# Row gathers of a retrieval layer: all query groups ahead of the first weighted sum, query weights in eight 1 MB loads

## The reference, cut to what matters

```python
def peer_ffn(xn, w_q, sub_keys, u, v):
    def block(xb):                                   # 128 tokens
        q = (xb @ w_q).reshape(PEER_BLOCK, PEER_HEADS, 2, PEER_HALF)
        s = jnp.einsum('thpd,hpnd->thpn', q, sub_keys).astype(jnp.float32)
        s_top, i_top = lax.top_k(s, PEER_TOPK)
        cand = s_top[:, :, 0, :, None] + s_top[:, :, 1, None, :]
        ...
        best, pos = lax.top_k(cand, PEER_TOPK)
        expert = jnp.take_along_axis(cand_idx, pos, axis=-1)
        g = jax.nn.softmax(best, axis=-1)
        act = jax.nn.gelu(jnp.einsum('td,thkd->thk', xb, u[expert]), approximate=False)
        return jnp.einsum('thk,thkd->td', (g * act).astype(xb.dtype), v[expert])
...
mem_kv = _rmsnorm(mem, norm_mem) @ w_mem_kv          # second layer, keys and values of the memory branch
```

## Time and profile before

| | us |
|---|---|
| median of 3 runs | 1346.45 (1339.59 to 1346.51) |
| the profiled execution | 1344.95 |
| its span on the core | 1343.2 |
| TensorE busy | 1111.8 |
| VectorE busy | 776.9 |
| ScalarE busy | 466.1 |
| GpSimd busy | 294.1 |
| granted clock of TensorE, mean | 0.928 of full |

### The profile page before, as it was taken

One profiled execution on the slowest core, in us unless ns is written; L12 is line 12 of the kernel. 1 busy time (PEld: TensorE's weight loads), 2 busy tenths in 40 slices (PEclk: granted clock), 3 DMA queues, 4 the chain that ended last, 5 costly groups with the idle time before them and its releaser, 6 DMA issues.

```text
span 1343.2 us, 13221 instructions
## 1 busy us (share of the span) xinstructions
PE 1111.8 (83%) x4936; PEld 745.6 (56%) x4936; DVE 776.9 (58%) x1528; ACT 466.1 (35%) x979; POOL 294.1 (22%) x313
## 2 busy tenths in 40 slices
PE   9999996749448677685976868676799999999997
PEld 9889784534213233232432323232498989888886
DVE  6587536123275665857567484344476664665665
ACT  5556211112032322322322232122448534465443
POOL 0052101130244433253342424133100000000001
PEclk9999998879779989799897979898899999999999
DMA  6453454356799999999999999999254423435533
GB/s 208 174 189 126 143 187 188 125 219 281 279 366 422 421 421 422 421 422 421 422 422 421 422 420 422 417 356 391 95 188 156 158 98 124 157 127 188 192 122 110
DMA packets 57665, 363.98 MB, mean 271 GB/s; under 512 B 6768, under 2 KB 9088, under 8 KB 16128
## 3 DMA queue, kind: packets, MB, share of 16 engines
q0 software_dynamic: 36864, 268.45, 48.6%
q1 hardware_dynamic: 20272, 94.48, 19.6%
q10 hardware_dynamic: 464, 0.20, 0.1%
HBM read 361.01 MB, written 2.10 MB: 270 GB/s over the span
## 4 chain that ended last, share of the span: by engine, by line
PE 59%; DMA 19%; DVE 12%; ACT 4%; POOL 3%; issue 2%; POOLq 0%; DVEq 0%; ACTq 0%
PE ps L2075 19%; PE ps L1912 18%; DMA big<-in_uv,big 11%; PE ps L1878 9%; DMA ring<-in_uv,big 4%; PE ps L1834 3%; DMA actT<-in_uv,big 2%; DVE big L1475 2%; PE ps L1963 2%; ACT big L993 1%; POOL ring L778 1%; POOL big L778 1%; PE ps L2025 1%; DVE lo L1270 1%; PE ps L1792 1%
## 5 line engine op out<-in xcount | busy, mean ns | idle before, releaser
L2075 PE MATMUL ps<-big 128*128 128x512 f32 x552 | 275.5, 647 | 124.3 <-ACT big L993 124.3
L2075 PEld LDWEIGHTS ps<-big 128*128 128x128 f32 x552 | 111.5, 206 | 278.0 <-ACT big L993 144.2
L1475 DVE CUSTOM_DVE_ANT_0 big<-big,ps 128x1024 f32<-128x1024 f32 x138 | 166.6, 1220 | 156.6 <-DMA big<-in_uv,big 154.1
L2075 PE MATMUL ps<-ring,big 128*128 128x512 f32 x336 | 166.5, 636 | 75.1 <-ACT big L993 69.4
L1912 PE MATMUL ps<-hi,x 128*128 128x512 f32 x704 | 227.0, 397 | 1.2 <-DVE lo L1270 1.0
L778 POOL DMA_INDIRECT big<-in_uv,big x138 | 131.0, 949 | 297.5 <-PE ps L2075 162.7
L985 ACT ACTIVATE big<-big 128x4 f32<-128x4 f32 x64 | 13.1, 205 | 487.6 <-DVE big L1475 487.6
L1270 DVE TENSOR_TENSOR lo<-raw,hi 128x2048 fp32r<-128x2048 f32 x60 | 139.2, 2321 | 74.1 <-ACT hi L859 73.8
L1475 DVE CUSTOM_DVE_ANT_0 ring<-ring,ps 128x1024 f32<-128x1024 f32 x84 | 101.9, 1220 | 138.0 <-DMA ring<-in_uv,big 138.0
L2075 PEld LDWEIGHTS ps<-ring,big 128*128 128x128 f32 x336 | 67.9, 206 | 168.8 <-issue 89.2
L1912 PEld LDWEIGHTS ps<-hi,x 128*128 128x128 f32 x704 | 133.7, 190 | 30.2 <-issue 2.2
(11 more groups left out here) (369 smaller groups left out, 1340.3 us busy)
## 6 DMA issues: line engine op xcount, KB each, us to landing
raw<-in_pieces SPq DMA_DIRECT2D x61, 1024.0 KB, 4.8
ring<-in_peer_w_q SPq DMA_DIRECT2D x4, 2048.0 KB, 8.0
big<-in_up SPq DMA_DIRECT2D x4, 2048.0 KB, 8.5
big<-in_uv,big POOLq DMA_INDIRECT x138
ring<-in_w_mem_kv SPq DMA_DIRECT2D x1, 2048.0 KB, 18.0
ring<-in_uv,big POOLq DMA_INDIRECT x84
resid<-in_x SPq DMA_DIRECT2D x2, 512.0 KB, 4.7
raw<-in_pieces SPq DMA_DIRECT2D x2, 512.0 KB, 8.9
```

The source lines that it names most:

```text
L1475: ins = dve.tensor_tensor_reduce(out=row, in0=row, in1=hn_ps[n], scale=1.0, scalar=0.0, op0=ALU.mult, op1=ALU.add, accum_out=dots[:, n, s: ...
L2075: ins = pe.matmul(ps[:, 4 + 2 * n + half, :], diag[:, s % DIAGS], row_home[home_of[k]][:, D + half * TILE:D + (half + 1) * TILE], start=(s ...
```

## The change

The query weights come as eight loads of 1 MB, one for each group, in three half slots of the ring (ring0, ring1, ring2) in turn: load i + 3 waits for group i. `mv` comes as two loads of 1 MB into ring0 and ring1. TensorE computes all eight query groups and their key scores before any weighted sum; from group 2 on the key scores come one group late, and the memory steps of groups 2 to 5 move behind, the last of them now after batch 7. ScalarE's hand-written order follows. The homes change: rows 4, 5 and 6 take ring3, ring4 and ring5, free since the output projection, row 7 takes ring2 (after group 5), row 8 actT (after group 7), rows 9 to 11 query0, query1 and keys (after the last key scores), row 24 mixT, rows 40 to 42 memT, ring0 and ring1 (after mv1), row 48 mkv; each other row takes the home that has been in use longest.

```diff
+WQ_HOMES = 3
...
-        tiles1 = [("wq0", wtile("peer_w_q", 0)), ("wq1", wtile("peer_w_q", TILE)),
-                  ("wq2", wtile("peer_w_q", 2 * TILE)), ("wq3", wtile("peer_w_q", 3 * TILE)),
-                  ("mv", wtile("w_mem_kv_2", TILE))]
...
+        def wq_view(i):
+            return ring_half[i % WQ_HOMES].rearrange("p (c n) -> p c n", c=KC)
+
+        def mv_view(c):
+            return ring_half[c // HALF].rearrange("p (c n) -> p c n", c=HALF)[:, c % HALF]
...
+        def query_used(i):
+
+            return group_done, group_no["wq00"] + i + 1
...
-        FIRST_ROW = {"early0": 0, "early1": 0, "early2": 0, "early3": 0, "ring4": 4, "ring5": 4, "ring0": 8, "ring1": 8, "actT": 8,
-                     "query0": 8, "query1": 8, "keys": 8, "mixT": 8, "memT": 24, "ring2": 24, "ring3": 24, "mkv": 32}
+        FIRST_ROW = {"early0": 0, "early1": 0, "early2": 0, "early3": 0, "ring3": 4, "ring4": 5, "ring5": 6, "ring2": 7,
+                     "actT": 8, "query0": 9, "query1": 10, "keys": 11, "mixT": 24, "memT": 40, "ring0": 40, "ring1": 41, "mkv": 48}
...
-            for k, (name, make) in enumerate(tiles1):
-                if k == 0:
-                    sp.wait_ge(piece_lo, NP1)
-                elif k == 1:
+            sp.wait_ge(piece_lo, NP1)
+            for i in range(PH):
+                if i == 2:
                     sp.wait_ge(wout_done, 4)
-                elif k >= RING:
-                    sp.wait_ge(*tile_used(tiles1[k - RING][0]))
-                dst, src = make(k % RING)
-                sp.dma_start(dst, src).then_inc(tile_loaded[k % RING], 16)
+                elif i >= WQ_HOMES:
+                    sp.wait_ge(*query_used(i - WQ_HOMES))
+                src = t["peer_w_q"][:, i * T:(i + 1) * T].rearrange("(c p) n -> p c n", p=P)
+                sp.dma_start(wq_view(i), src).then_inc(query_then_mv_loaded[i % WQ_HOMES], 16)
+            for k in range(2):
+                sp.wait_ge(*query_used(PH - 2 + k))
+                sp.dma_start(ring_half[k].rearrange("p (c n) -> p c n", c=HALF), w_mem[:, HALF * k:HALF * (k + 1), TILE:2 * TILE]).then_inc(query_then_mv_loaded[k], 16)
...
+            mv_used = (group_done, group_no["mv1"] + 1)
+            home_ready = {"ring3": (wout_done, 4), "ring4": (wout_done, 4), "ring5": (wout_done, 4), "ring2": query_used(5),
+                          "actT": query_used(PH - 1), "query0": (sub_done, PH), "query1": (sub_done, PH), "keys": (sub_done, PH),
+                          "mixT": (group_done, group_no["mk1"] + 1), "memT": mv_used, "ring0": mv_used, "ring1": mv_used, "mkv": (hq0a_then_mkv_moved, 32)}
...
             for i in range(PH):
                 out_query(i)
-                out_scores(i)
-                if i == 2:
+                if i == 3:
                     exponentials(0)
-                if i == 4:
+                if i >= 3:
+                    out_scores(i - 1)
+                elif i < 2:
+                    out_scores(i)
+                if i == PH - 2:
                     exponentials(1)
-                    weigh(0)
-                if i == 6:
-                    weigh(1)
-            out_memory("mk1")
-            for b in range(2, BATCHES):
+            out_scores(PH - 1)
+            for b in range(BATCHES):
                 weigh(b)
                 if b == 4:
+                    out_memory("mk1")
+                if b == 6:
                     out_memory("mv0")
-                if b == 6:
+                if b == 8:
                     out_memory("mv1")
...
             for i in range(PH):
-                features(f"wq{i // 2}", actT, (i % 2,))
-                if i < 6:
+                query_features(i)
+                if i < 2:
                     memory(19 + 2 * i, 21 + 2 * i)
-                if i == 0:
-                    pe.wait_ge(cols_then_mem_loaded, 96)
-                key_scores(i)
-                if i == 4:
-                    weighted_rows(0)
-                if i == 6:
-                    weighted_rows(1)
-            memory(31, 32)
-            for b in range(2, BATCHES):
+                    if i == 0:
+                        pe.wait_ge(cols_then_mem_loaded, 96)
+                    key_scores(i)
+                elif i > 2:
+                    key_scores(i - 1)
+            memory(23, 25)
+            key_scores(PH - 1)
+            for b in range(BATCHES):
                 weighted_rows(b)
-                if b < 6:
-                    memory(24 + 4 * b, 28 + 4 * b)
+                if b == 2:
+                    memory(25, 28)
+                if 3 <= b < 8:
+                    memory(4 * b + 16, 4 * b + 20)
```

More of the change, by code:

```diff
@@ L222, in build @@
         memT_done = sem("memT_done")
-        tile_loaded = [sem(f"tile_loaded{i}") for i in range(RING)]
+        tile_loaded = [sem(f"tile_loaded{i}") for i in range(2)]
+        query_then_mv_loaded = [sem(f"query_then_mv_loaded{i}") for i in range(WQ_HOMES)]
         consts_made = sem("consts_made")
@@ L269, in build @@
         t["mkv_keep"] = nc.dram_tensor("mkv_keep", (P, 2048), F32, kind="Internal").ap()
[L272 to L284 removed]
+        loads_p = [len(range(s, NP1, 2)) for s in range(2)]
         tokens_of = ["hi", "gv", "hgate", "ggate", "wo0", "wo1", "dnz", "gmu", "gmv", "gmz", "swz", "xmz"]
@@ L304, in piece_loads @@
             k, s = load_no[name], raw_slot(name)
-            return 16 * (k // 2 + 1 if k < NP1 else loads1[s] + (k - NP1) // 2 + 1)
+            return 16 * (k // 2 + 1 if k < NP1 else loads_p[s] + (k - NP1) // 2 + 1)
         def raw_piece(name):
@@ L318, in build @@
         up_order = [(k % 2, k // 2) for k in range(4)]
-        def slot(name):
-            return tile_no[name] % RING
-        def tile_view(name):
-            return ring[:, slot(name), :].rearrange("p (c n) -> p c n", c=KC)
+        ring_half = [ring[:, k // 2, (k % 2) * 2 * D:(k % 2 + 1) * 2 * D] for k in range(6)]
+        def wq_view(i):
+            return ring_half[i % WQ_HOMES].rearrange("p (c n) -> p c n", c=KC)
+        def mv_view(c):
+            return ring_half[c // HALF].rearrange("p (c n) -> p c n", c=HALF)[:, c % HALF]
         groups1 = ["hq0", "hq1", "hf0", "hf1", "gqk0", "gqk1", "glow", "hi0", "hi1", "gv0", "gv1",
@@ L372, in build @@
         EARLY = 15872
-        ring_half = [ring[:, k // 2, (k % 2) * 2 * D:(k % 2 + 1) * 2 * D] for k in range(6)]
         row_home = {f"early{k}": big[:, EARLY + 2 * D * k:EARLY + 2 * D * (k + 1)] for k in range(3)}
         row_home["early3"] = past_actT[:]
-        for k in (4, 5, 0, 1):
+        for k in (3, 4, 5, 2):
             row_home[f"ring{k}"] = ring_half[k]
@@ L1813, in transpose_to_tiles @@
                             ins.then_inc(transposed, 1)
-            def need(name):
-                pe.wait_ge(tile_loaded[slot(name)], 16 * (loads_p[slot(name)] + tile_no[name] // RING + 1))
             def bank_free(g):
@@ L1822, in bank_free, with query_features @@
                     pe.wait_ge(group_out, same[-1] + 1)
-            def features(name, xT, subs):
-                need(name)
-                w = tile_view(name)
-                for s in subs:
-                    g = f"{name}{s}"
-                    bank_free(g)
-                    for a in range(2):
-                        f0 = (2 * s + a) * P
-                        for c in range(KC):
-                            ins = pe.matmul(ps[:, gbank(g), a * T:(a + 1) * T], w[:, c, f0:f0 + P], xT[:, c, :], start=(c == 0), stop=(c == KC - 1))
-                    ins.then_inc(group_done, 1)
-            def tokens(name, xT):
-                need(name)
-                w = tile_view(name)
-                for n in range(NT):
-                    g = f"{name}{n}"
-                    bank_free(g)
+            def query_features(i):
+                pe.wait_ge(query_then_mv_loaded[i % WQ_HOMES], 16 * (i // WQ_HOMES + 1))
+                w = wq_view(i)
+                g = f"wq{i // 2}{i % 2}"
+                bank_free(g)
+                for a in range(2):
                     for c in range(KC):
-                        ins = pe.matmul(ps[:, gbank(g), :], xT[:, c, n * P:(n + 1) * P], w[:, c, :], start=(c == 0), stop=(c == KC - 1))
-                    ins.then_inc(group_done, 1)
+                        ins = pe.matmul(ps[:, gbank(g), a * T:(a + 1) * T], w[:, c, a * P:(a + 1) * P], actT[:, c, :], start=(c == 0), stop=(c == KC - 1))
+                ins.then_inc(group_done, 1)
             FRESH = {"hq0": 0, "dnq0": 16}
@@ L2018, in memory @@
                         if g == "mv0":
-                            need("mv")
+                            for half in range(2):
+                                pe.wait_ge(query_then_mv_loaded[half], 16 * (len(range(half, PH, WQ_HOMES)) + 1))
                     if k < 32:
@@ L2024, in memory @@
                         n = (k - 32) // KC
-                        ins = pe.matmul(ps[:, gbank(g), :], memT[:, c, n * P:(n + 1) * P], tile_view("mv")[:, c], start=(c == 0), stop=(c == KC - 1))
```

(1 more changed line is left out.)

16 lines of the change are left out of this document (1 added, 15 removed).

## The result

The changed kernel takes 1287.42 us, median of 4 runs (1284.83 to 1290.32), beside 1346.48 us for the kernel before, also 4 runs (1339.59 to 1347.63). The ratio is 0.9572, 95% interval 0.9532 to 0.9613. The profiled run of the changed kernel took 1285.52 us with a span of 1283.8 us, 59.4 us less than the span of before.

The account below looks back on a forecast made before the run. Gather bytes at 421 GB/s were taken as the bound. From 259.5, 607.6 for 244 rows, 2.5 store, 1.5 dark and 20.4 tail gave 891.5, 61.3 us sooner; span 1282 and 1.75 around it, forecast 1285 us, range 1272 to 1302.

Parts of the forecast that it names:

- The bound: Whole gather stretch: once gathers run at full rate, only their bytes count, 2.49 us a row at 421 GB/s.
- Dark time as the measure: Gather stretch: time the DMA engines stand idle sets the gain, 77.0 us before and 13.8 after.
- Rival 2: Query loads starve beside the gathers: load 6 also late, group 6 slips some 9 us, 1294 us; chance 0.06.
- Load 7: Last query-weight load, issued beside rows 0 to 6: lands with the last queued byte at 232.3, costing 2.4 us.
- Group 7: Last query group on TensorE: ends at 239.2 after the late load; row 8 issued at 239.5.
- The first sum: First weighted sum: TensorE idle 4.5 us, then slow at 9.4 us; ends 256.0, row 12 issued at 256.3.
- Rows 40 and 48: Gathers waiting for mv1 and the mkv store: the only close releases, 1.5 us dark taken.
- Rival 1: Loop on 12 to 16 homes runs dry: 10 to 25 us given back, 1295 to 1310; chance 0.11.
- The end: Last dot product on VectorE: at 891.5 where before has 952.8, a gain of 61.3 us.
- Rival 3: Row 8 or 12 stays held back, only the front dark time shrinks: 1335 us or no gain; chance 0.03.
- Rival 5: Loop bound by its round trip in all units, 11.2 us a batch against 9.96: 1360 us; chance 0.02.
- Rival 4: Better than forecast: load 7 on time (2.4), first sum warm (2.5), shorter last-row gaps (5): 1275 us; chance 0.06.

Follow-up runs that it names:

- half of the sums: Changed kernel with 56 of 64 batches multiplying only the first 512 of 1024 columns of the weighted sum; 1280.57 us.
- half of the bytes: Changed kernel with rows 64 to 191 gathering only their u half, 0.52 MB each, all instructions kept; 1213.2 us.
- the first weigh early: Changed kernel with ScalarE doing weigh(0) before it copies out the last query group; 1280.81 us.

## Why the prediction was right

*The bound.* Right, and shown from two sides: half of the sums don't change the rate, half of the bytes do change the time.

*Dark time as the measure.* Right. The prediction counted 77.0 us of it before and 13.8 after; measured in the same way for all kernels it is 75.5 and 15.4, and the last dot product follows it within 3 us in eleven kernels. The kernel with the order undone brings the dark stretches and 28 us back.

*TensorE up to group 6, and query loads up to 6.* Right: group 6 starts at 220.18 with no wait, and the loads take 5.5 us in the median. Rival 2 (load 6 starves too) is out.

*Load 7.* The prediction let it land with the last byte of its neighbours, at 232.3, from the row of mv; it landed at 233.5, and the engines are dark from 234.3, so with the last bytes it was. But row 0 had left 1.55 us early: from there load 7 took until 28.4 us, where 25.6 was predicted. And it isn't the place in the queue that decides but the short runs, as the long ones show with 9.1 us beside the same rows. The prediction's remark that turns fit only if a turn of the gathers is the larger one is borne out; that the layout of the load could change it was not seen. Equal shares, 8 us, which the prediction set against its own figure, would have been near for long runs.

*Group 7.* Here a term was missed. The wait of 2.4 us was counted and the group behind it was costed warm, at 6.91 us. The wait was 5.38 us (the load 1.2 us later, TensorE ready 1.8 us earlier, at 228.1), the granted clock in 235 to 240 us stood at 0.61, and the group took 9.84. The prediction asked of the first sum whether it would run cold, and not of the group. With that and the later landing, row 8 left at 243.63 in place of 239.5.

*The first sum.* Right in kind and size: the GELU table load (1.28 us, at 246.81 on ScalarE) came to lie on the path, TensorE waited 4.40 us (4.5 predicted), and the clock was cold. Start at 250.56 in place of 246.6, row 12 at 260.66 in place of 256.3. Since row 0 left 1.55 us earlier than before, that is 5.9 us more from row 0 to row 12 than predicted.

*Rows 40 and 48.* No dark stretch where 1.5 us was put: the DMA share is 0.98 from 330 to 335 and 0.97 from 340 to 345. Rival 1 is out, though the slices say how near it was.

*The end.* The last dot product started at 892.30, where 891.5 was predicted. Late by 4.4 at row 12, late by 0.8 here: 3.6 us were made good. Some 1.5 of them are the pause that did not come; 422 for 421 GB/s over 244 rows makes up to 1.4. What is left, under a microsecond, fits the last 80 us, dark for 7.1 us in place of 8.3. So the forecast of 1285 us was met to 2.4 us partly by luck: a missed cost of some 3 us for the cold group met a tail and pauses that were put too high by as much, and row 0 left 1.55 us earlier than in the profile of before. Counted from row 0, the last dot product came 58.9 us sooner where 61.3 were forecast.

*The rivals.* Rival 3 (only the early bursts count) needed a dark stretch that stayed, and the full rate from 262 us on leaves no room for one. Rival 5 needed batches slower than 10.96 us: at 422 GB/s they come every 9.94 us, and the loop's own round with half the bytes is 62.6 / 8 = 7.8 us a batch. Rival 4, each part of it on time, didn't happen by itself, but two of its parts could be had by an edit, and each was worth more than it put. Load 7 on time, put at 2.4 us, brought the last dot product 7.7 to 8.1 us forward, 3.6 of which the cold group alone gives. The first sum warm, put at 2.5, came with its wait gone, 6.0 together. The third part, shorter gaps in the last rows, is what the half sums touch, 3 us.

## What to carry to other kernels

Where the transfers bind, count the time in which their engines are dark and ask for each dark stretch which release it waits for and what stands ahead of that on its engine; work that waits for data doesn't belong ahead of work that frees buffers. A load in short runs that was issued beside large gathers came late far beyond its bytes: issue it before them, or lay it out in long runs. And a wait of some microseconds put on TensorE can cost twice, since what runs behind it can be cold (5.38 us of waiting were followed by a group that took 2.8 us more); ask it of every stage behind a wait.

## What the runs showed of the hardware

- 1 MB in runs of 1 KB lands in 5.3 to 5.5 us alone, and in 21.8 us beside gathers of 1 MB each (six issued by then, two more on the way) with runs of 8 KB; in runs of 8 KB it lands in 9.1 us beside the same gathers.
- TensorE idle for 4.40 us ran its next twelve matmuls slowly (8.11 us where a warm first sum took 5.32); 3.61 us had been harmless. But 3.61 us are no safe length: a little later in the changed kernel 3.38 us of idling were followed by twelve slow matmuls, and with the first weigh early 2.40 us by four in 3.58 us (warm: 1.88) at a granted clock of 0.50. What ran ahead of these pauses differs, so no limit is read from them.

```profile
278.80 7.11 PE L2054 MATMUL ps<-big 128*128 128x512 f32 x12 [3.38 <-ACT big L985]
```

- Data flows sooner after an issue than the prediction took it: after the issue of row 12 at 260.66 the engines are busy 0.84 of the microsecond from 262 to 263, so within some 1.5 us. The 3.2 us of the prediction, from issue to the dot product less 2.49, hold the completion as well.

```profile
262.00:263.00 1.00, 1.00 (x4) 0.51 (x3) 0.00 (x0) 0.21 (x1) 0.83 (x1) 1.00 0.84 139
```
